# The second mixer's block inverse on packed 32x32 diagonal blocks, four products side by side in the array

## Chip, core and metric

One Trainium2 chip, one of its cores, one launch. The engines are PE (TensorE, matrix products into PSUM), DVE (VectorE), ACT (ScalarE), POOL (GpSimd) and SP (which issues most DMAs). Each runs its own instruction list in order and they meet only at semaphores. The metric is the device time of one launch in microseconds; lower is better.

## What is computed

Two transformer blocks on 256 tokens of width 1024, in float32. The change touches one part of the second block, the RWKV-7 mixer, whose core is a recurrence for each of 8 heads of width 64:

```
def step(state, inp):
    r_t, w_t, k_t, v_t, a_t, b_t = inp
    sa = jnp.einsum('bhvk,bhk->bhv', state, a_t)
    state = (state * w_t[:, :, None, :]
             + sa[..., :, None] * b_t[:, :, None, :]
             + v_t[..., :, None] * k_t[:, :, None, :])
    y_t = jnp.einsum('bhvk,bhk->bhv', state, r_t)
    return state, y_t
```

The kernel works in chunks of 64 tokens. Within a chunk the rows `sa` depend on each other through a strictly triangular 64x64 matrix M (one for each head and chunk), and are had at once by the inverse of I - M, a unit triangular matrix.

## The kernel before, in words

There are 4 chunks and 8 heads, so 32 matrices of 64x64. Two heads share the 128 partitions (head h on partitions 64h to 64h+63), so they lie as 16 units side by side: `m_b` holds M, `x_inv` and `xt_inv` hold the growing inverse and its transpose, both 128 x 16 x 64.

The inverse is grown by levels. At level 0 DVE sets `xt_inv` to the 2x2 blocks of M on the diagonal plus the identity (two operations, L1074 and L1077), PE turns it into `x_inv` (L578) and ACT copies that out of PSUM. At level n (1 to `LEVELS` = 5) blocks of size 2^n are joined in pairs: with N the part of M between the two (M times a mask in `levels`, by POOL, L1433, into `half_n`), P = N X (`first_product`), then X += X P and Xᵀ += Pᵀ Xᵀ (`second_product`). Level 5 needs only the transposed one. Every product is done for two halves f of 8 units, through `product` (L588): 8 units times 2 heads, so 16 matmuls of 64x64 with 64 columns into one PSUM bank. A head's matmul uses the 64 rows and the 64 columns of the array that its partitions stand for. In float32 a matmul shows as two records in the trace.

Round it goes PE -> ACT (P out of bank 4 into `half_1`, L861) -> PE -> DVE (`grow`: adds to `x_inv`, L1088, and `xt_inv`, L1091) -> PE. So that PE has something to do meanwhile, the level loop weaves in pieces of wide projections (`columns(...)`, L2196 to L2198, 3 matmuls of 128x128 by 256 columns for each step): after `first_product(n, 0)` stands `second_product(n - 1, 1)`, then `second_product(n, 0)`, `first_product(n, 1)`, and a piece of `columns`. These wide matmuls need each chunk of weights in two parts, which ACT (`split`, L1464, `w_hi`) and DVE (`split`, L1766, `w_lo`) make, in their own order between the level's operations. After the inverse comes the recurrence over chunks (L657), which uses `xt_inv`.

The masks are made once by POOL in `second_constants`, in the first block.

Of the kernel before, what the change touches and what calls it, by code (L numbers as in the profile page):

```python
# [10 lines left out]
ALU = mybir.AluOpType  # L11
ACT = mybir.ActivationFunctionType
# [26 lines left out]
NCH = T // CHUNK  # L39
LORA = 160  # L40
# [48 lines left out]
def block_pair(nc, inp, out, scratch, shifted):  # L89

    ctx = ExitStack()
    with ctx:
# [249 lines left out]
        x_inv, xt_inv = region(4096, NCH * HT, CHUNK), region(5120, NCH * HT, CHUNK)  # L342
        m_b, m_k = region(6144, NCH * HT, 2 * CHUNK), region(9216, NCH * HT, 2 * CHUNK)
        b_tok, k_tok, v_tok = (region(11264 + 1024 * j, NCH * HT, CHUNK) for j in range(3))
        half_1, half_n = region(14336, 2, 8 * CHUNK), region(15360, 2, 8 * CHUNK)
# [9 lines left out]
        levels = sb("levels", [P, 6, CHUNK])  # L355
        eye = sb("eye", [P, CHUNK])
# [37 lines left out]
        LEVELS = 5  # L394
        FUNITS = HT * TT
# [7 lines left out]
        def second_constants(told, pool, g):  # L403
# [20 lines left out]
            for h in range(2):  # L424
                a, b = HD * h, HD * (h + 1)
                g.tensor_copy(eye[a:b, :], ident[a:b, a:b]).then_inc(S["pool_step"], told.one("pool_step"))
                pool.wait_ge(S["pool_step"], told.value("pool_step"))
# [6 lines left out]
            for n in range(LEVELS + 1):  # L434
                w = 2 ** n
                both = levels[:, n, :].rearrange("p (b t) -> p b t", t=2 * w)
                g.memset(both[:, :, w:2 * w], 1.0).then_inc(S["pool_step"], told.one("pool_step"))
                pool.wait_ge(S["pool_step"], told.value("pool_step"))
                for h in range(2):
                    v = both[HD * h:HD * (h + 1)]  # L440
                    blocks = CHUNK // (2 * w)
# [4 lines left out]
                    done = "masks_ready" if n == LEVELS and h else "pool_step"  # L446
# [13 lines left out]
        def head(v, h, *rest):  # L460
            return v[(slice(HD * h, HD * (h + 1)), *rest)]


        def pe_mixer(told, pe, state, by_columns, by_tokens, by_rows, rows_to_tokens, turn_late_half, spread):
# [111 lines left out]
            for u in range(NCH * HT):  # L576
                for h in range(2):
# [7 lines left out]
            def product(b, left, right, f):  # L585
                for i in range(8):
                    for h in range(2):
# [4 lines left out]
            def x_of(f, i, h):  # L592
                return head(x_inv, h, 8 * f + i)

            def xt_of(f, i, h):
                return head(xt_inv, h, 8 * f + i)

            def n_of(f, i, h):
                return head(half_n, h, f, slice(i * CHUNK, (i + 1) * CHUNK))

            def p_of(f, i, h):
                return head(half_1, h, f, slice(i * CHUNK, (i + 1) * CHUNK))

            def first_product(n, f):

                done = 2 * (n - 1) + f
                pe.wait_ge(S["off_ready"], done + 1)
# [4 lines left out]
                product(4, n_of, x_of, f).then_inc(S["p1"], told.one("p1"))  # L612

            def second_product(n, f):

                done = 2 * (n - 1) + f
                pe.wait_ge(S["p1_copied"], done + 1)
                if n > 1:
                    pe.wait_ge(S["xt_added"], done - 1)
                if n < LEVELS:  # L620
                    product((6, 5)[f], xt_of, p_of, f)
                product((7, 3)[f], p_of, xt_of, f).then_inc(S["p2"], told.one("p2"))

            pe.wait_ge(S["turned_copied"], 8)
            pe.wait_ge(S["turned_copied"], 6)
# [20 lines left out]
            for c in range(NCH):  # L646
# [140 lines left out]
        def act_mixer(told, act, a, split, spread, state):  # L787
# [59 lines left out]
            copies("units_turned", 4, x_inv, 6, "turned_copied")  # L847
# [86 lines left out]
        def dve_mixer(told, dve, v, split, diagonals, out_bank, state):  # L934
# [139 lines left out]
            v.tensor_tensor(xt_inv, m_b[:, :, 0:CHUNK], over(levels[:, 0, :], NCH * HT), ALU.mult).then_inc(  # L1074
                S["dve_step"], told.one("dve_step"))
            dve.wait_ge(S["dve_step"], told.value("dve_step"))
            v.tensor_tensor(xt_inv, xt_inv, over(eye[:], NCH * HT), ALU.add).then_inc(  # L1077
# [5 lines left out]
            def grow(n, f):  # L1083

                dve.wait_ge(S["p2"], 2 * (n - 1) + f + 1)
                if n < LEVELS:
                    o = flat(x_inv[:, 8 * f:8 * f + 8, :])
                    v.tensor_tensor(o, o, bank[(6, 5)[f]][:, :], ALU.add).then_inc(  # L1088
                        S["x_added"], told.one("x_added"))
                o = flat(xt_inv[:, 8 * f:8 * f + 8, :])  # L1090
                v.tensor_tensor(o, o, bank[(7, 3)[f]][:, :], ALU.add).then_inc(  # L1091
                    S["xt_added"], told.one("xt_added"))

            dve.wait_ge(S["turned_copied"], 8)
# [235 lines left out]
        def _(pool):  # L1330
# [97 lines left out]
            pool.wait_ge(S["xt_first"], 1)  # L1428
            for n in range(1, LEVELS + 1):
                for f in range(2):  # L1430
                    if n > 1:
                        pool.wait_ge(S["p1"], 2 * (n - 2) + f + 1)
                    g.tensor_tensor(half_n[:, f, :].rearrange("p (u s) -> p u s", u=8),  # L1433
                                    m_b[:, 8 * f:8 * f + 8, 0:CHUNK], over(levels[:, n, :], 8), ALU.mult).then_inc(
                        S["off_ready"], told.one("off_ready"))

# [1121 lines left out]
```

## Time and profile before

| | us |
|---|---|
| median of 3 runs | 1129.97 (1129.5 to 1130.15) |
| the profiled execution's own time | 1129.57 |
| its span in the trace | 1127.7 |
| PE busy | 1116.1 (99%) |
| DVE busy | 768.8 (68%) |
| ACT busy | 559.5 (50%) |
| POOL busy | 183.4 (16%) |
| mean granted TensorE clock (share of 2.4 GHz) | 0.998 |

Times in the trace are microseconds from the span's start. A busy PE is a PE with a matmul in its pipeline; neighbouring matmuls overlap, so the time that one takes from the stream is the distance between starts, not its duration. The inverse lies between 752 and 803 us.

### The profile page before, as it was taken

How to read it: one execution, taken by the hardware profiler on the slowest of the kernel's cores; microseconds unless marked ns; L12 is line 12 of the kernel's file. 1: busy time of each engine (PE TensorE's matmuls, PEld its weight loads, DVE VectorE, ACT ScalarE, POOL GpSimd, SP SyncE). 2: the span in 40 equal slices, each digit the busy share in tenths (PEclk: the TensorE clock that was granted, in tenths of full speed). 3: DMA queues.
4: the chain of work that ended last, by engine and by line, in shares of the span. 5: the costliest groups of instructions: out<-in, count | busy, mean ns of one | idle time of the engine just before them, and what ended most of it. 6: DMA issues, size and time to landing. Idle time of an engine off the chain costs nothing.

```text
span 1127.7 us, 22169 instructions
## 1 busy us (share of the span) xinstructions
PE 1116.1 (99%) x9610; PEld 1058.4 (94%) x9610; DVE 768.8 (68%) x1033; ACT 559.5 (50%) x671; POOL 183.4 (16%) x127
## 2 busy tenths in 40 slices
PE   9999999999999999999999999999999999999997
PEld 9999999998999999899999999999998989999996
DVE  4988978757786776775555567974278675554554
ACT  6433344494754554674444448622245656343343
POOL 3888783000000000000000010113030010000000
PEclk9999999999999999999999999999999999999999
DMA  8586553355456555546456565433144354655551
GB/s 271 188 289 201 184 187 112 117 211 174 138 197 203 201 170 186 178 147 215 156 186 210 161 202 157 129 92 99 41 142 136 136 182 155 205 185 187 187 185 39
DMA packets 147150, 190.01 MB, mean 168 GB/s; under 512 B 7659, under 2 KB 132139, under 8 KB 146943
## 3 DMA queue, kind: packets, MB, share of 16 engines
q1 hardware_dynamic: 145743, 184.32, 50.2%
q0 software_dynamic: 1264, 4.55, 1.2%
q8 instruction: 59, 0.97, 0.4%
q14 instruction: 20, 0.16, 0.0%
q10 hardware_dynamic: 64, 0.02, 0.0%
HBM read 187.79 MB, written 2.65 MB: 169 GB/s over the span
## 4 chain that ended last, share of the span: by engine, by line
PE 94%; DVE 3%; ACT 2%; issue 1%; ACTq 0%; DVEq 0%
PE bank L2196 22%; PE bank L2197 21%; PE bank L2198 21%; PE bank L2348 6%; PE bank L2349 6%; PE bank L2350 6%; PE bank L588 2%; PE bank L657 1%; DVE w_lo L1766 1%; PE bank L2280 1%; PE bank L2276 1%; PE bank L2436 1%; PE bank L562 1%; PE bank L2450 1%; PE bank L475 0%
## 5 line engine op out<-in xcount | busy, mean ns | idle before, releaser
L2196 PE MATMUL bank<-X_hi,w_hi 128*128 128x256 f32 x1760 | 502.5, 286 | 0.6 <-DVE w_lo L1766 0.5
L2197 PE MATMUL bank<-X_lo,w_hi 128*128 128x256 f32 x1760 | 497.9, 283 | 0.0
L2198 PE MATMUL bank<-X_hi,w_lo 128*128 128x256 f32 x1760 | 497.9, 283 | 0.0
L1464 ACT ACTIVATE w_hi<-w_raw 128x2048 fp32r<-128x2048 f32 x170 | 324.0, 1909 | 149.6 <-PE bank L2198 112.4
L1766 DVE TENSOR_TENSOR w_lo<-w_raw,w_hi 128x2048 fp32r<-128x2048 f32 x144 | 332.4, 2311 | 42.4 <-ACT w_hi L1464 42.0
L2196 PEld LDWEIGHTS bank<-X_hi,w_hi 128*128 128x128 f32 x1760 | 337.3, 192 | 6.3 <-issue 2.6
L2197 PEld LDWEIGHTS bank<-X_lo,w_hi 128*128 128x128 f32 x1760 | 337.4, 192 | 1.2
L2198 PEld LDWEIGHTS bank<-X_hi,w_lo 128*128 128x128 f32 x1760 | 337.3, 192 | 0.0
L1893 DVE TENSOR_TENSOR arena<-bank,rstd 128x512 f32<-128x512 f32 x66 | 45.6, 691 | 184.3 <-PE bank L2198 179.5
L1373 POOL TENSOR_TENSOR w_lo<-w_raw,w_hi 128x2048 fp32r<-128x2048 f32 x23 | 106.8, 4650 | 33.0 <-ACT w_hi L1464 32.9
L2348 PE MATMUL bank<-w_hi,Y_hi 128*128 128x512 f32 x264 | 103.3, 391 | 1.2 <-DVE Y_lo L1921 1.2
L2349 PE MATMUL bank<-w_hi,Y_lo 128*128 128x512 f32 x264 | 103.1, 390 | 0.0
L2350 PE MATMUL bank<-w_lo,Y_hi 128*128 128x512 f32 x264 | 102.7, 389 | 0.0
L1415 POOL TENSOR_TENSOR w_lo<-w_raw,w_hi 128x2048 fp32r<-128x2048 f32 x2 | 9.2, 4596 | 537.4 <-ACT w_hi L1464 537.4
L1998 DVE SCALAR_TENSOR_TENSOR bank<-arena,par,bank 128x256 f32<-128x256 f32 x232 | 93.2, 482 | 0.6
L2348 PEld LDWEIGHTS bank<-w_hi,Y_hi 128*128 128x128 f32 x264 | 49.7, 188 | 11.1 <-DVE Y_lo L1921 1.6
L2350 PEld LDWEIGHTS bank<-w_lo,Y_hi 128*128 128x128 f32 x264 | 49.6, 188 | 10.6
L1574 ACT ACTIVATE arena<-arena,par 128x256 f32<-128x256 f32 x44 | 24.1, 595 | 69.4 <-DVE arena L1893 69.4
L2349 PEld LDWEIGHTS bank<-w_hi,Y_lo 128*128 128x128 f32 x264 | 49.7, 188 | 9.1
L1583 ACT ACTIVATE arena<-arena 128x512 f32<-128x512 f32 x22 | 13.9, 633 | 84.4 <-DVE arena L1893 84.4
L1597 ACT ACTIVATE Y_hi<-arena 128x512 fp32r<-128x512 f32 x33 | 20.9, 632 | 44.0 <-DVE arena L1914 44.0
L1803 DVE TENSOR_TENSOR arena<-bank,rstd 128x512 f32<-128x512 f32 x43 | 29.5, 687 | 13.7 <-PE bank L2198 9.9
(302 smaller groups left out, 1404.5 us busy)
## 6 DMA issues: line engine op xcount, KB each, us to landing
w_raw<-in_ffn_w_dram SPq DMA_DIRECT2D x66, 1024.0 KB, 5.4
w_raw<-in_w_in_dram SPq DMA_DIRECT2D x52, 1024.0 KB, 5.2
w_raw<-in_w_up_dram SPq DMA_DIRECT2D x22, 1024.0 KB, 5.1
w_raw<-in_w_down_dram SPq DMA_DIRECT2D x11, 1024.0 KB, 4.9
w_raw<-in_w_out_dram SPq DMA_DIRECT2D x8, 1024.0 KB, 5.1
w_raw<-in_conv_pw_w_dram SPq DMA_DIRECT2D x4, 1024.0 KB, 5.1
w_raw<-in_w_attn_out_dram SPq DMA_DIRECT2D x2, 1024.0 KB, 4.9
w_raw<-in_rwkv_proj_dram SPq DMA_DIRECT2D x2, 1024.0 KB, 4.9
```

Of the source, the lines that this page charges most:

```text
L1373: g.tensor_tensor(w_lo[n % RING][:, :], raw[n % RING][:, :], w_hi[n % RING][:, :].bitcast(F32), ALU.subtract).then_inc(S["w_lo_pool"], tol ...
L1464: a.activation(w_hi[slot][:, :], raw[slot][:, :], ACT.Copy).then_inc(S["w_hi"], told.one("w_hi"))
L1766: v.tensor_tensor(w_lo[slot][:, :], raw[slot][:, :], w_hi[slot][:, :].bitcast(F32), ALU.subtract).then_inc(S["w_lo"], told.one("w_lo"))
L1803: v.tensor_tensor(dst, pairs(b), over(rstd[:], 2), ALU.mult).then_inc(S[f"bank{b}_read"], 1)
L1893: v.tensor_tensor(u_t[:, side].rearrange("p (m t) -> p m t", m=2), pairs(2 * (i % 2) + side), over(rstd[:], 2), ALU.mult).then_inc(S[name] ...
L1998: v.scalar_tensor_tensor(out=conv[:, t, :] if k == CONV_W - 1 else part, in0=src, scalar=w, in1=part, op0=ALU.mult, op1=ALU.add).then_inc( ...
L2196: pe.matmul(o, wh, xh, start=start, stop=False, skip_group_check=True)
L2197: pe.matmul(o, wh, xl, start=False, stop=False, skip_group_check=True)
L2198: return pe.matmul(o, wl, xh, start=False, stop=stop, skip_group_check=True)
L2348: pe.matmul(o, yh, wh, start=first and k == 0, stop=False, skip_group_check=True)
L2349: pe.matmul(o, yl, wh, start=False, stop=False, skip_group_check=True)
L2350: mm = pe.matmul(o, yh, wl, start=False, stop=last, skip_group_check=True)
```

## The change

The inverse is grown to 32x32 only, on packed diagonal blocks, and the last level is done apart.

- Each 64x64 matrix has two 32x32 blocks on the diagonal. They lie on partitions 32q to 32q+31 (q = 0 to 3; two heads, two blocks each). POOL copies them out of `m_b` into a new `m_blocks` (128 x 16 x 32), 8 copies of 32 partitions by 256 elements. `x_blocks` and `xt_blocks` (128 x 16 x 32) replace `x_inv` and, up to level 4, `xt_inv`.
- Levels 1 to 4 run on these. `product` now makes, for each unit, 4 matmuls of 32x32 with 32 columns, each on its own 32 rows and its own 32 columns of the array, instead of 2 of 64x64 with 64 columns. The copies, adds and masks around them have half as many elements for each partition.
- Level 5 is `corner_product`: the 32x32 corner between the two blocks, 2 matmuls of 32x32 for each unit and product, no mask. DVE copies the corner into `xt_inv` (2 copies of 32 partitions for each half f in place of one add); POOL clears the opposite corner and copies the diagonal blocks into `xt_inv` (2 memsets, 8 copies). The recurrence waits for these at chunks 0 and 2.
- The turn before level 1 becomes 64 matmuls of 32x32 in place of 32 of 64x64, into one bank, and ACT copies one bank in place of two.
- The masks are 32 wide: 5 levels by 4 quarters in place of 6 levels by 2 halves.

```diff
-            for u in range(NCH * HT):
-                for h in range(2):
-                    mm = pe.matmul(head(bank[6 + u // 8], h, slice(u % 8 * CHUNK, u % 8 * CHUNK + CHUNK)),
-                                   head(xt_inv, h, u), head(ident, h, slice(HD * h, HD * (h + 1))),
-                                   start=True, stop=True)
+                for q in range(QUADRANTS):
+                    mm = pe.matmul(quadrant(bank[6], q, slice(u * BLOCK, (u + 1) * BLOCK)), quadrant(xt_blocks, q, u),
+                                   quadrant(ident, q, slice(q * BLOCK, (q + 1) * BLOCK)), start=True, stop=True)
...
             def product(b, left, right, f):
                 for i in range(8):
+                    for q in range(QUADRANTS):
+                        mm = pe.matmul(quadrant(bank[b], q, slice(i * BLOCK, (i + 1) * BLOCK)), left(f, i, q),
+                                       right(f, i, q), start=True, stop=True)
+                return mm
...
+            def corner_product(b, left, right, below, f):
+                for i in range(8):
                     for h in range(2):
-                        mm = pe.matmul(head(bank[b], h, slice(i * CHUNK, (i + 1) * CHUNK)), left(f, i, h),
-                                       right(f, i, h), start=True, stop=True)
+                        mm = pe.matmul(quadrant(bank[b], 2 * h + below, slice(i * BLOCK, (i + 1) * BLOCK)),
+                                       left(f, i, h), right(f, i, 2 * h + 1 - below), start=True, stop=True)
                 return mm
...
+                if c % 2 == 0:
+                    pe.wait_ge(S["off_ready"], 2 * QUADRANTS + 2 * (LEVELS - 1) + QUADRANTS * (c // 2 + 1))
...
-                    a.activation(half_1[:, f, :], bank[4][:, :], ACT.Copy).then_inc(
+                    a.activation(half_1[:, f, :], bank[4][:, 0:T], ACT.Copy).then_inc(
...
+            dve.wait_ge(S["off_ready"], 2 * QUADRANTS)
+            v.tensor_tensor(xt_blocks, m_blocks, over(levels[:, 0, :], NCH * HT), ALU.mult).then_inc(
...
+                    for h in range(2):
+                        done = "xt_added" if h else "dve_step"
+                        v.tensor_copy(quadrant(xt_inv, 2 * h, slice(8 * f, 8 * f + 8), slice(BLOCK, CHUNK)),
...
+            for f in range(2):
+                pool.wait_ge(S["masked"], 4 * f + 3)
+                for q in range(QUADRANTS):
+                    g.tensor_copy(quadrant(m_blocks, q, units(f)), quadrant(m_b, q, units(f), diagonal_block(q))).then_inc(
+                        S["off_ready"], told.one("off_ready"))
...
+            for f in range(2):
+                pool.wait_ge(S["xt_added"], 2 * (LEVELS - 2) + f + 1)
+                for q in range(QUADRANTS):
+                    g.tensor_copy(quadrant(xt_inv, q, units(f), diagonal_block(q)),
+                                  quadrant(xt_blocks, q, units(f))).then_inc(S["off_ready"], told.one("off_ready"))
```

What this makes of the instruction lists, at two places. First PE in level 2, before: the four lines are `first_product(2, 0)`, `second_product(1, 1)`, `second_product(2, 0)` and `first_product(2, 1)`, each with its first matmul apart.

```order
3916 L588 MATMUL bank<-arena 64x64 [waits x_added,p1_copied,off_ready]
3917 L588 MATMUL bank<-arena 64x64 x15
3918 L588 MATMUL bank<-arena 64x64 [waits p1_copied]
3919 L588 MATMUL bank<-arena 64x64 x31
3920 L588 MATMUL bank<-arena 64x64 [waits xt_added,p1_copied]
3921 L588 MATMUL bank<-arena 64x64 x31
3922 L588 MATMUL bank<-arena 64x64 [waits x_added,p1_copied,off_ready]
3923 L588 MATMUL bank<-arena 64x64 x15
```

And the same place of the changed kernel:

```order
3916 L597 MATMUL bank<-arena 32x32 [waits x_added,p1_copied,off_ready]
3917 L597 MATMUL bank<-arena 32x32 x31
3918 L597 MATMUL bank<-arena 32x32 [waits p1_copied]
3919 L597 MATMUL bank<-arena 32x32 x63
3920 L597 MATMUL bank<-arena 32x32 [waits xt_added,p1_copied]
3921 L597 MATMUL bank<-arena 32x32 x63
3922 L597 MATMUL bank<-arena 32x32 [waits x_added,p1_copied,off_ready]
3923 L597 MATMUL bank<-arena 32x32 x31
```

Order and waits stay; there are twice as many matmuls, each a quarter of the size. The second place is POOL round the inverse. Before (L1415 is a weight split in the first block's feed-forward part, L1433 the masks times M, L1439 the forgetting rows of the attention):

```order
94 L1426 DMA bias_by_distance<-arena 8x256 [waits forget]
95 L1433 TENSOR_TENSOR arena<-arena,levels 128x512 [waits xt_first]
96 L1433 TENSOR_TENSOR arena<-arena,levels 128x512
97 L1433 TENSOR_TENSOR arena<-arena,levels 128x512 [waits p1] x8
98 L1439 DMA arena<-bias_by_distance 128x2048 [waits y_summed,forget_stored]
```

After:

```order
108 L1466 DMA bias_by_distance<-arena 8x256 [waits forget]
109 L1479 COPY arena<-arena 32x256 [waits masked]
110 L1479 COPY arena<-arena 32x256 x3
111 L1479 COPY arena<-arena 32x256 [waits masked]
112 L1479 COPY arena<-arena 32x256 x3
113 L1486 TENSOR_TENSOR arena<-arena,levels 128x256 [waits off_ready]
114 L1486 TENSOR_TENSOR arena<-arena,levels 128x256
115 L1486 TENSOR_TENSOR arena<-arena,levels 128x256 [waits p1] x6
116 L1492 MEMSET arena 32x16x32 [waits off_ready,xt_first]
117 L1492 MEMSET arena 32x16x32
118 L1498 COPY arena<-arena 32x8x32 [waits xt_added,pool_step]
119 L1498 COPY arena<-arena 32x8x32 x3
```

Eight copies now stand ahead of the first mask, and DVE's first two operations of the inverse, which waited only for PE and ACT before, wait for them as well; eight more copies and two memsets stand behind the last mask.

## Rows read from the trace of the kernel before

**Rows 1.** The page: busy time of PE, and the chain that ended last.
```profile
PE 1116.1 (99%) x9610; PEld 1058.4 (94%) x9610; DVE 768.8 (68%) x1033; ACT 559.5 (50%) x671; POOL 183.4 (16%) x127
...
PE 94%; DVE 3%; ACT 2%; issue 1%; ACTq 0%; DVEq 0%
```

**Rows 2.** Timeline of PE: start us, us, engine, line, operation, shapes, records.
```profile
754.98 2.08 PE L578 MATMUL bank<-ident,arena 64*64 64x64 f32 x64
756.99 0.39 PE L2196 MATMUL bank<-X_hi,w_hi 128*128 128x256 f32 x1
...
759.34 1.15 PE L588 MATMUL bank<-arena 64*64 64x64 f32 x32
760.42 0.39 PE L2196 MATMUL bank<-X_hi,w_hi 128*128 128x256 f32 x1
...
766.62 5.82 PE L588 MATMUL bank<-arena 64*64 64x64 f32 x192
772.36 0.39 PE L2196 MATMUL bank<-w_hi,X_hi 128*128 128x256 f32 x1
...
803.26 14.41 PE L657 MATMUL bank<-arena 64*64 64x64 f32 x432
```

**Rows 3.** Timeline of PE elsewhere: other shapes and pairs of tiles (rows*columns of the array).
```profile
692.84 0.37 PE L515 MATMUL bank<-arena 32*128 32x256 f32 x1
692.84 0.37 PE L517 MATMUL bank<-arena 32*128 32x256 f32 x1
...
721.62 0.61 PE L540 MATMUL bank<-ident,arena 8*128 8x8 f32 x4
...
741.34 7.20 PE L562 MATMUL bank<-arena 64*64 64x128 f32 x128
...
819.94 1.89 PE L697 MATMUL bank<-arena,head_ones 128*128 128x256 f32 x8
```

**Rows 4.** Timeline of ACT, of the inverse and of the recurrence behind it.
```profile
764.39 0.60 ACT L861 ACTIVATE arena<-bank 128x512 f32<-128x512 f32 x1 [3.26 <-PE bank L588]
764.88 1.91 ACT L1464 ACTIVATE w_hi<-w_raw 128x2048 fp32r<-128x2048 f32 x1
...
803.99 0.38 ACT L868 ACTIVATE arena<-bank 128x256 f32<-128x256 f32 x1 [1.77 <-PE bank L657]
```

**Rows 5.** Timeline of DVE: the first steps of the inverse, level 2, a 128x256 add.
```profile
749.32 2.29 DVE L1766 TENSOR_TENSOR w_lo<-w_raw,w_hi 128x2048 fp32r<-128x2048 f32 x1
751.52 0.68 DVE L1803 TENSOR_TENSOR arena<-bank,rstd 128x512 f32<-128x512 f32 x1
...
753.65 1.23 DVE L1077 TENSOR_TENSOR arena<-arena,eye 128x1024 f32<-128x1024 f32 x1
...
766.82 2.29 DVE L1766 TENSOR_TENSOR w_lo<-w_raw,w_hi 128x2048 fp32r<-128x2048 f32 x1 [2.02 <-ACT w_hi L1464]
769.03 0.68 DVE L1803 TENSOR_TENSOR arena<-bank,rstd 128x512 f32<-128x512 f32 x1
769.75 0.69 DVE L1088 TENSOR_TENSOR arena<-arena,bank 128x512 f32<-128x512 f32 x1
...
810.35 0.42 DVE L1107 TENSOR_TENSOR arena<-arena,bank 128x256 f32<-128x256 f32 x1 [3.54 <-PE bank L657]
```

**Rows 6.** Timeline of POOL: the masks of the inverse, and two places in the first block.
```profile
156.62 0.74 POOL L1395 TENSOR_TENSOR sq<-sq 128x256 f32<-128x256 f32 x1
...
183.14 4.14 POOL L1403 TENSOR_TENSOR sq<-sq 128x512 f32<-128x512 f32 x3 [6.41 <-ACT sq L1470]
...
760.58 1.29 POOL L1433 TENSOR_TENSOR arena<-arena,levels 128x512 f32<-128x512 f32 x1 [1.05 <-PE bank L588]
...
767.86 2.38 POOL L1433 TENSOR_TENSOR arena<-arena,levels 128x512 f32<-128x512 f32 x1 [2.12 <-PE bank L588]
```

**Rows 7.** Stretch 735 to 805 us: busy us (records); its instruction queue: packets, MB.
```profile
735.00:805.00 70.00, 69.98 (x1533) 67.62 (x1533) 39.25 (x49) 18.75 (x27) 16.42 (x10) 1.00 0.29 91
...
q8 instruction: 12, 0.20, 1.2%
```

More of the change, by code:

```diff
@@ L39 @@
 NCH = T // CHUNK
+BLOCK = 32
 LORA = 160
@@ L433, in second_constants @@
                     pool.wait_ge(S["pool_step"], told.value("pool_step"))
-            for n in range(LEVELS + 1):
+            for q in range(QUADRANTS):
+                c = slice(BLOCK * q, BLOCK * (q + 1))
+                g.tensor_copy(eye[c, :], ident[c, c]).then_inc(S["pool_step"], told.one("pool_step"))
+            pool.wait_ge(S["pool_step"], told.value("pool_step"))
+            for n in range(LEVELS):
                 w = 2 ** n
@@ L438, in second_constants @@
                 pool.wait_ge(S["pool_step"], told.value("pool_step"))
[L439 to L441 removed]
+                for q in range(QUADRANTS):
+                    v = both[BLOCK * q:BLOCK * (q + 1)]
+                    blocks = BLOCK // (2 * w)
                     g.affine_select(out=v, in_=v, compare_op=ALU.is_ge, fill=0.0, base=0,
@@ L445, in second_constants @@
                     pool.wait_ge(S["pool_step"], told.value("pool_step"))
-                    done = "masks_ready" if n == LEVELS and h else "pool_step"
+                    done = "masks_ready" if n == LEVELS - 1 and q == QUADRANTS - 1 else "pool_step"
                     g.affine_select(out=v, in_=v, compare_op=ALU.is_ge, fill=0.0, base=w - 1,
@@ L611, in first_product @@
                     pe.wait_ge(S["x_added"], done - 1)
-                product(4, n_of, x_of, f).then_inc(S["p1"], told.one("p1"))
+                if n < LEVELS:
+                    mm = product(4, n_of, x_of, f)
+                else:
+                    mm = corner_product(4, corner_of, x_of, 1, f)
+                mm.then_inc(S["p1"], told.one("p1"))
             def second_product(n, f):
@@ L621, in second_product @@
                     product((6, 5)[f], xt_of, p_of, f)
-                product((7, 3)[f], p_of, xt_of, f).then_inc(S["p2"], told.one("p2"))
-            pe.wait_ge(S["turned_copied"], 8)
-            pe.wait_ge(S["turned_copied"], 6)
+                    mm = product((7, 3)[f], p_of, xt_of, f)
+                else:
+                    mm = corner_product((7, 3)[f], p_below, xt_of, 0, f)
+                mm.then_inc(S["p2"], told.one("p2"))
+            pe.wait_ge(S["turned_copied"], 7)
             pe.wait_ge(S["forget_read"], 1)
@@ L846, in act_mixer @@
             copies("units_turned", 3, v_tok, 4, "turned_copied")
-            copies("units_turned", 4, x_inv, 6, "turned_copied")
+            act.wait_ge(S["units_turned"], 4)
+            a.activation(flat(x_blocks), bank[6][:, :], ACT.Copy).then_inc(
+                S["turned_copied"], told.one("turned_copied"))
             def v_tokens(j):
@@ L1073, in dve_mixer @@
             dve.wait_ge(S["units_turned"], 2)
-            v.tensor_tensor(xt_inv, m_b[:, :, 0:CHUNK], over(levels[:, 0, :], NCH * HT), ALU.mult).then_inc(
+            dve.wait_ge(S["off_ready"], 2 * QUADRANTS)
+            v.tensor_tensor(xt_blocks, m_blocks, over(levels[:, 0, :], NCH * HT), ALU.mult).then_inc(
                 S["dve_step"], told.one("dve_step"))
             dve.wait_ge(S["dve_step"], told.value("dve_step"))
-            v.tensor_tensor(xt_inv, xt_inv, over(eye[:], NCH * HT), ALU.add).then_inc(
+            v.tensor_tensor(xt_blocks, xt_blocks, over(eye[:], NCH * HT), ALU.add).then_inc(
                 S["xt_first"], told.one("xt_first"))
@@ L1432, in _ @@
                         pool.wait_ge(S["p1"], 2 * (n - 2) + f + 1)
-                    g.tensor_tensor(half_n[:, f, :].rearrange("p (u s) -> p u s", u=8),
-                                    m_b[:, 8 * f:8 * f + 8, 0:CHUNK], over(levels[:, n, :], 8), ALU.mult).then_inc(
+                    g.tensor_tensor(half_n[:, f, :].rearrange("p (u s) -> p u s", u=8), m_blocks[:, units(f), :],
+                                    over(levels[:, n, :], 8), ALU.mult).then_inc(
                         S["off_ready"], told.one("off_ready"))
+            pool.wait_ge(S["xt_first"], 1)
+            pool.wait_ge(S["off_ready"], told.value("off_ready"))
+            for h in range(2):
+                g.memset(quadrant(xt_inv, 2 * h + 1, slice(0, NCH * HT), slice(0, BLOCK)), 0.0).then_inc(
+                    S["pool_step"], told.one("pool_step"))
+            pool.wait_ge(S["pool_step"], told.value("pool_step"))
+            for f in range(2):
+                pool.wait_ge(S["xt_added"], 2 * (LEVELS - 2) + f + 1)
+                for q in range(QUADRANTS):
+                    g.tensor_copy(quadrant(xt_inv, q, units(f), diagonal_block(q)),
+                                  quadrant(xt_blocks, q, units(f))).then_inc(S["off_ready"], told.one("off_ready"))
             pool.wait_ge(S["forget_stored"], 16)
```

63 lines of the change are left out of this document (39 added, 24 removed).

## The prediction

> **What bounds the kernel now.** I read the page's busy times and the chain that ended last first [rows 1]: PE is busy for 99% of the span and holds 94% of the chain, so what leaves PE's stream shortens the launch, and what happens on DVE, ACT and POOL counts only where PE comes to wait for it. Then PE's timeline through the inverse [rows 2]. The blocks of small matmuls and the wide ones follow each other without a hole: the block of level 2 (192 records) starts at 766.62, and the next wide matmul at 772.36, 5.74 us later; a block of 32 records takes 760.42 - 759.34 = 1.08 us. So a record costs (5.74 - 1.08) / 160 = 29.1 ns and a block 1.08 - 32 x 0.0291 = 0.15 us for going in and out. Each record has a partner, the other head's, so I count in steps: one pass of all tiles of a unit. A step is 58.3 ns. The records of L588 are 896, so 448 steps; the turn (L578) has 64 records, 32 steps. In all 480 steps and 28.0 us of step time, everything else being wide matmuls that stay.
>
> **What a step costs after.** The number of steps does not change. In levels 1 to 4 (384 steps) and in the turn (32) a step now has four tiles in place of two, and the corner level (64 steps) has two tiles, all 32x32 with 32 columns. So the change is worth 480 times the difference between 58.3 ns and the new step P, and P is the number to find. No row has a 32x32 tile with 32 columns. Three shapes bound it [rows 2, 3]:
> - 64 weight columns, 64 moving columns: 58 ns (L588).
> - 64 weight columns, 128 moving columns: (7.20 - 0.15) / 64 = 110 ns for a pair (L562).
> - 128 weight columns, 8 moving columns: (0.61 - 0.25) / 3 = 120 ns, where 0.25 is my estimate for the last one's pipeline time (L540).
>
> So the larger of the two counts sets the time, by 0.052 us for each 64 columns above 58 ns. Halving both should take off half of that, 26 ns: P = 32 ns. That is so if four tiles overlap as two do. For the two: L515 and L517 stand on different rows of the array and start at the same 692.84 [rows 3], and a pair of L562 with 128 columns each takes 110 ns, where one matmul of the full array needs (1.89 - 0.38) / 7 = 216 ns for 256 columns, 108 for 128 (L697) [rows 3]. Two tiles thus cost what one costs. Four are not in the trace. The lower bound is P = 27, half of the bare 53 ns by which the other shapes differ; the upper is that records come no denser than the densest stream of this trace, one in 29.1 ns, 116 ns for four and 58 for two. I take 32, as the stagger in a pair is too small to be seen in rows of a hundredth of a microsecond, so four fit in.
>
> A rule that speaks against this: the Trainium skill, in "TensorEngine Tiling (Array Packing)", under "Restrictions and Gotchas", says that different row tiles cannot access the same PSUM bank at the same time, and all four quarters write one bank here. By it four would be done one after another, and the step would be 4 x 32 = 128 ns. But L562's and L588's two heads are different row tiles and share a bank, and the 110 ns for two speaks against it, as long as they write different partitions.
>
> **The sum on PE.** 480 x (58.3 - 32) = -12.6 us: the turn -0.8, levels 1 to 4 -10.1, the corner -1.7. The 9 blocks keep their 0.15 us each.
>
> **What may now wait.** The cover is shorter, so I put the loop on a clock again.
> - ACT's copy of P has half the elements: 0.38 us in place of 0.60 [rows 4]. It begins some 0.2 us after the last matmul of `first_product(n, 0)`, and is covered by `second_product(n - 1, 1)`, 32 steps or 1.0 us: 0.6 needed, no wait. At level 1 the cover is 0.9 us of wide matmuls, enough.
> - DVE's adds take 0.42 us each in place of 0.69 [rows 5]. `first_product(n, 1)` needs `x_added` of (n - 1, 1), with `second_product(n, 0)` between, 1.0 us: 0.2 + 0.42 needed, no wait by themselves.
> - But between the adds DVE has `split`, and at level 1 also L1803. From ACT's split at 764.88 to DVE's split (766.82), L1803 (769.03) and the add at 769.75 with its end at about 770.4 [rows 4, 5], it is one chain of 5.5 us, and only 0.25 us of it shrinks. It starts when ACT has copied P of (1, 1). New clock: the turn starts at 754.98 as before and ends 0.8 earlier, so level 1's first block starts at 758.5 and lasts 16 x 0.032 + 0.15 = 0.66 us (before 1.08). With the same 0.9 us of wide matmuls the second block (48 steps) starts at 760.1 and ends at 761.8. ACT's copy follows at 761.9, its split at 762.2, and the chain's add is done at 762.2 + 5.25 = 767.5. PE: 2.35 us of wide matmuls, level 2's block from 764.1, and the 80 steps ahead of `first_product(2, 1)` end at 764.1 + 0.1 + 2.6 = 766.8. PE waits **0.8 us** there. Before, this add was done at 770.4 and PE came to it at 766.62 + 0.1 + 80 x 0.058 = 771.4. Levels 3 and 5 have no L1803 in the chain, and their chain starts 3 us of wide matmuls ahead; it ends with the last product of the level's first half or before it: no wait. This is what is late next; if P is lower, it grows by a step's difference times 80.
> - POOL, now ahead of DVE's first two steps. The copies for the first half of the units run before 748, the second four start at about 748.5 (when the last `m_b` is masked). A 128x256 operation on POOL takes 0.74 us with two inputs; I estimate 0.5 for a copy. POOL does not get on while DVE makes a `w_lo`: L1433 took 2.38 us at 767.86, when DVE's split ran to 769.1, and 1.29 at 760.58, when none did [rows 5, 6]. DVE's split from 749.32 to 751.6 [rows 5] thus pushes two or three of the four copies behind it: done at 752.6 to 753.2, against 752.4, when DVE was ready before. The masks of level 1 now follow at once on POOL, 0.74 us each, and can hold DVE up in turn. Against this DVE's two operations take half of 1.23 us each [rows 5]. They ended at 754.88 and would now end between 754.0 and 755.6; PE wants them at 754.98. I take **0.3 us** (0 to 1).
> - At the end PE went from the last block over 0.9 us of wide matmuls into the recurrence at 803.26 [rows 2]. The last block is short now, and DVE has two copies of about 0.4 us in place of one add of 0.69: **0.1 us**.
> - The copies into `xt_inv` on POOL: the first four can start in level 4, the second in level 5, some 5 us ahead of the recurrence for 2 us of work (4 x 0.5). Hidden by that; uncovered it would be up to 2 us.
> - Masks on POOL in the first block: 50 operations where there were 36, smaller ones. The 6.41 us for which POOL waited at 183.14 [rows 6] cover them.
> - Behind the inverse PE and the splits keep their distances, so what is won stays won.
>
> Sum: -12.6 + 0.8 + 0.3 + 0.1 = -11.4 us, from 1129.57 for the profiled execution 1118.2; the median of the runs lies 0.4 higher, so **1118.6 us**. Own range of this case: 1115 (P = 27 and a longer wait at level 2) to 1121.
>
> **Rivals.**
> 1. *Four tiles do not come as densely as two.* For each step of four PE needs four weight loads and four matmuls in 32 ns, twice as many instructions for each step as now and near four times the present rate. Nothing in the trace shows PE fed at that rate. The instruction queue moved 12 packets of 0.20 MB in these 70 us for 1533 matmul records, 128 each, in 1.2% of 16 engines' time, so 1.1 us each [rows 7]; a level's block of 384 records would now want 3 of them in 3.1 us, just what one queue gives. Halfway, P = 45 for the 416 steps of four: 416 x 13 = 5.4 us less gain, but the wait at level 2 goes too: 1123.5. Chance 0.17, range 1121 to 1128.
> 2. *PE takes a record at a time at a fixed pace* (the other side). That the present 29.1 ns for a record were a pace, not 64 columns, is against L562's 55 ns and the shared starts of L515 and L517, yet no row has a denser stream. Then four tiles cost 116 ns and two stay at 58: 416 x 58.3 = +24.3, no gain at the corner, no waits: 1154. It turns from gain to loss at P = 62 for four (with the corner's 1.7 us kept). Chance 0.12, range 1132 to 1154. The Trainium skill has a floor of that kind, in "TensorE: Matmul & The Clock Gate", section "Wait — 56ns, not 53.3ns?": starts never closer than about 25 ns, however few the columns. By it a step of four would be 100 ns, and the time 416 x 42 = 17 us above 1130, about 1147. L515 and L517, with one start on different rows of the array, speak against it between tiles.
> 3. *Only two tiles overlap.* Four make 2 x 32 = 64 ns: 416 x 5.7 = +2.4, the corner -1.7: 1130.7, no change. The present pairs are all that the trace shows. Chance 0.07.
> 4. *Waits eat more*: DVE and POOL take turns at more places than I counted, and each level's adds come late by a microsecond: 1123. It falls in the range of rival 1; chance 0.06.
>
> **How the numbers follow.** The likeliest case has 0.58 and gives 1118.6. The range leaves out rival 2 and half of the third: 1114.5 to 1130.5. A change under 0.2% (2.3 us) is about what a measurement of this kernel can't tell from none. Faster: the first case, 1 and 4, 0.81, less 0.03 for the tail of 1: 0.78. Same: 0.03 and most of rival 3: 0.09. Slower: 0.13.
>
> **What would show it.** In the trace of the changed kernel the block of level 2 to 4 should take 96 x 0.032 + 0.15 = 3.2 us where it took 5.74 (level 2 with a hole of 0.8 us before its last quarter, levels 3 and 4 without). L588's successor has 1664 records, in blocks of 0.66 us (64 records) and 1.0 us in the corner level. DVE's second step of the inverse ends by 755.6. ACT's copies take 0.38 us. If the block takes over 5.7 us, rival 2 or 3 holds; if it is between 3.5 and 5 without a wait named, rival 1; if waits of PE for DVE stand at every level, rival 4. I am wrong, too, if the wide matmuls take longer than before, or if the gain is there at 803 us and gone at the end.

## The result and the profile after

| | before | after |
|---|---|---|
| median, us | 1130.06 (6 runs) | 1150.19 (6 runs, 1147.27 to 1152.62) |
| profiled execution, us | 1129.57 | 1149.05 |
| its span, us | 1127.7 | 1147.0 |
| mean granted TensorE clock | 0.998 | 0.987 |

The changed kernel is slower: the ratio of the times is 1.018, 95% interval 1.017 to 1.019. That is 20 us lost where 11 us of gain were forecast.

Nearly all of it lies in the inverse: 18.2 of the 19.3 us by which the two profiled spans differ. From the turn to the recurrence PE took 803.26 - 754.98 = 48.3 us before; after, it takes 822.15 - 755.65 = 66.5. The 0.67 us by which the later trace starts the inverse late are there at 742 us already, and behind the recurrence the two run alike to 0.4 us.

PE's timeline shows what no row of before has, a stream that breaks off. These are the small matmuls of levels 1 to 3 (L597 is `product`, L588's successor; the last bracket is the idle time ahead, "issue" meaning that PE waited for nothing that the profile shows). They answer to the L588 rows of [rows 2]:

```profile
765.29 1.32 PE L597 MATMUL bank<-arena 32*32 32x32 f32 x128 [0.43 <-issue]
768.59 0.63 PE L597 MATMUL bank<-arena 32*32 32x32 f32 x40 [1.98 <-issue]
...
772.86 1.95 PE L597 MATMUL bank<-arena 32*32 32x32 f32 x197
777.15 1.35 PE L597 MATMUL bank<-arena 32*32 32x32 f32 x127 [2.33 <-issue]
780.72 1.06 PE L597 MATMUL bank<-arena 32*32 32x32 f32 x60 [2.23 <-issue]
```

A full piece between two holes has 127 or 128 records, whatever product it belongs to. While a piece runs, it runs as forecast: 128 records, 32 steps of four tiles, in 1.32 us less about 0.19 for the last one's pipeline time, 35 ns a step. Then PE has nothing to do for some 2 us. PE's list of waits between 741 and 830 us (us in total, times, longest) says it in three lines; the kernel before has no line at all in this list between 741 and 811 us:

```profile
PE bank L597 <- issue: 15.7, 8, 3.6
PE bank L588 <- issue: 2.2, 1, 2.2
PE bank L2260 <- issue: 0.7, 1, 0.7
```

The wide matmuls behind a hole are slow too. Before, their starts are 0.12 us apart and each lasts 0.28; these are the first ones behind level 2's block:

```profile
781.72 0.58 PE L2260 MATMUL bank<-w_hi,X_hi 128*128 128x256 f32 x1
782.10 0.42 PE L2261 MATMUL bank<-w_lo,X_hi 128*128 128x256 f32 x1
782.31 0.41 PE L2262 MATMUL bank<-w_hi,X_lo 128*128 128x256 f32 x1
```

They start 0.21 us apart. The stretches of the two kernels from the turn to the recurrence (columns: stretch, then busy us and records of PE, PE's weight loads, DVE, ACT and POOL, granted clock, DMA share, GB/s) first after, then before:

```profile
754.98:822.15 67.17, 48.52 (x1943) 45.51 (x1942) 18.65 (x27) 12.35 (x20) 8.57 (x16) 0.80 0.24 76
```

```profile
754.98:803.26 48.28, 48.28 (x1106) 46.48 (x1105) 22.49 (x24) 14.46 (x20) 16.39 (x10) 1.00 0.32 98
```

PE is idle for 18.7 us of it, and the granted clock has a mean of 0.80: with levels 2.4 and 1.2 GHz that is 40% of the stretch at 1.2. Summing the distances between PE's starts by kind gives the whole account. A hole is counted here from the start of the last matmul ahead of it to the next start, so each is about 0.2 us longer than the idle time in brackets:

| us in this stretch | before | after | difference |
|---|---|---|---|
| small matmuls | 28.0 | 18.2 | -9.8 |
| holes | 0 | 20.6 | +20.6 |
| wide matmuls | 17.1 | 24.4 | +7.3 |
| going in and out of blocks | 3.2 | 3.3 | +0.1 |
| sum | 48.3 | 66.5 | +18.2 |

### The profile page after: what moved, and what is told of

Its sections match the earlier page's. It is cut to its first block, busy times and chain, and to the rows that moved or that the text cites. A ratio compares the mean times of both kernels' runs of the same rounds, so it can differ in the third digit from the quotient of the medians.

```text
span 1147.0 us, 23869 instructions
## 1 busy us (share of the span) xinstructions
PE 1116.3 (97%) x10442; PEld 1057.6 (92%) x10442; DVE 764.8 (67%) x1035; ACT 556.7 (49%) x670; POOL 187.1 (16%) x160
## 4 chain that ended last, share of the span: by engine, by line
PE 93%; DVE 3%; issue 2%; ACT 2%; ACTq 0%; DVEq 0%
PE bank L2260 21%; PE bank L2261 21%; PE bank L2262 21%; PE bank L2412 6%; PE bank L2413 6%; PE bank L2414 6%; PE bank L597 2%; PE bank L686 1%; DVE w_lo L1830 1%; PE bank L2344 1%; PE bank L2340 1%; PE bank L2500 1%; PE bank L572 1%; PE bank L2514 1%; PE bank L485 0%
## 5 line engine op out<-in xcount | busy, mean ns | idle before, releaser
L1957 DVE TENSOR_TENSOR arena<-bank,rstd 128x512 f32<-128x512 f32 x66 | 45.6, 691 | 184.2 <-PE bank L2262 179.4
L2414 PEld LDWEIGHTS bank<-w_lo,Y_hi 128*128 128x128 f32 x264 | 49.6, 188 | 10.5
L2260 PE MATMUL bank<-w_hi,X_hi 128*128 128x256 f32 x128 | 39.3, 307 | 0.7 <-issue 0.7
```

The lines of the kernel that those rows point to most:

```text
L1957: v.tensor_tensor(u_t[:, side].rearrange("p (m t) -> p m t", m=2), pairs(2 * (i % 2) + side), over(rstd[:], 2), ALU.mult).then_inc(S[name] ...
L2260: pe.matmul(o, wh, xh, start=start, stop=False, skip_group_check=True)
L2414: mm = pe.matmul(o, yh, wl, start=False, stop=last, skip_group_check=True)
```

## The experiments

Two theories of the holes. S: PE's instructions are supplied at a limited pace, 128 matmul records a packet, and four tiles use them up faster. T: the tiles; PE cannot keep four 32x32 tiles at work, or it stops after some number of them. A third question is the clock: do the holes lower it (C1), or the small tiles (C2)?

### Four tiles where nothing else is going on

```diff
             feed(2)
+            pe.wait_ge(S["tile_summed"], told.value("tile_summed"))
+            for i in range(160):
+                for q in range(4):
+                    pe.matmul(bank[1][32 * q:32 * (q + 1), i % 8 * 32:i % 8 * 32 + 32], ident[32 * q:32 * (q + 1), 32 * q:32 * (q + 1)],
+                              ones[32 * q:32 * (q + 1), 0:32], start=True, stop=True)
```

> The kernel before with 160 steps of four 32x32 tiles (1280 records) put on PE behind its last product, where nothing waits for it and the DMA queues move only the output. Theory S: the burst runs at about 9 ns a record for as long as instructions are at hand (one or two packets, 128 to 256 records), then stops every 128 records for about 2 us; 1280 records last about 10 x 3.6 = 36 us less the first, so the launch ends 25 to 30 us later, and the instruction packets come 3.5 us apart although no weights are moved. If the holes of the changed kernel came from DMA traffic or from its waits on other engines, the burst runs without holes, 12 us.

Measured: 1158.51 us, one run. PE's timeline (columns as above) has the same pieces and holes behind the kernel's last product, with no semaphore in between and no weights on the way (the output, 1.05 MB, is written in the first 9 us):

```profile
1120.68 2.12 PE L2538 MATMUL bank<-ones,ident 32*32 32x32 f32 x229
1125.45 1.27 PE L2538 MATMUL bank<-ones,ident 32*32 32x32 f32 x128 [2.65 <-issue]
1130.29 1.93 PE L2538 MATMUL bank<-ones,ident 32*32 32x32 f32 x128 [3.57 <-issue]
...
1145.06 1.93 PE L2538 MATMUL bank<-ones,ident 32*32 32x32 f32 x128 [1.55 <-issue]
1148.54 1.93 PE L2538 MATMUL bank<-ones,ident 32*32 32x32 f32 x128 [1.55 <-issue]
```

From 1145.06 to 1148.54 it is 3.48 us a piece. The granted clock is 1.00 up to 1125 us and 0.50 from 1130 us on, so a late piece runs for 1.93 us where the one at 1125.45 took 1.27. The DMA queues between 1120 and 1157 us (packets, MB, share of 16 engines' time):

```profile
GB/s 0 111 173 18 0 120 383 334 31 0 0 0 18 0 0 0 18 0 0 0 18 0 0 0 18 0 0 0 18 0 0 0 18 0 0 18 0 0 0 0
...
q8 instruction: 9, 0.15, 1.7%
```

In the line of 40 slices of 0.93 us, once the output is written (the peak at 383), one slice in four shows 18 GB/s: one packet of 16 KB for each piece of 128 records. Nine packets in 1.7% of 16 engines' 37 us are 1.1 us each. The trace has the times of single packets too, and with them the 3.48 us come apart. The piece at 1145.06 starts; 1.1 us later, at 1146.17, the next packet starts and is under way for 0.93 us; 1.4 us after its end, at 1148.54, the next piece starts. So a packet sets off only when PE has begun on the one before it. The changed kernel does the same in its stretch from 803 to 811 us, where no weights are on the way (40 slices of 0.2 us):

```profile
GB/s 0 0 0 0 0 0 0 0 82 0 0 0 0 0 0 0 0 0 0 0 0 0 0 0 0 82 0 0 0 0 0 0 0 0 0 0 0 0 0 0
...
q8 instruction: 2, 0.03, 1.5%
```

Its pieces start at 803.62 and 806.90, the two packets at 804.72 and 808.01, again 1.1 us behind. The first of these pieces runs at full clock, and it is 3.28 us to the next: the pace is 3.3 to 3.5 us a packet.

The same times settle what ends a hole. In the changed kernel all ten end 1.2 to 1.5 us after the end of an instruction packet. In this run and in the three further ones below that keep the small tiles of levels 1 to 4 it is 1.2 to 1.6 us for all 32 that the profile puts to "issue". Where PE waits for ACT instead (the run with ACT held, below), the last packet had ended 0.8, 4.4, 2.4, 1.5 and 7.5 us before. Nothing of the changed kernel's waits, of its transfers or of its other engines is needed for the holes.

### As many instructions in tiles of 64x64

```diff
+            for i in range(320):
+                for h in range(2):
+                    pe.matmul(bank[1][64 * h:64 * (h + 1), i % 8 * 64:i % 8 * 64 + 64], ident[64 * h:64 * (h + 1), 64 * h:64 * (h + 1)],
+                              ones[64 * h:64 * (h + 1), 0:64], start=True, stop=True)
```

> The kernel before with 320 steps of two 64x64 tiles (1280 records, as many instructions as in the burst of four tiles) put on PE behind its last product. Theory S: at 58.3 ns a step 128 records take 3.73 us, longer than the 3.5 us in which a packet comes, so there is no hole and the burst takes 320 x 0.058 = 18.7 us (the clock stays full), about 11 us past the end of before, near 1141. If any long run of small matmuls brings holes, the launch ends at 1158 as with four tiles.

Measured: 1159.79 us, one run. The burst has no hole, as S says, and its length was worked out wrongly in the expectation: 1280 records of two tiles are 640 steps, not 320, so 37.3 us. The time alone would have spoken for the other side (1158 us); it is the trace that decides.

```profile
1120.15 37.55 PE L2538 MATMUL bank<-ones,ident 64*64 64x64 f32 x1280
...
q8 instruction: 10, 0.16, 1.8%
```

(Timeline, and the instruction queue from 1120 to 1158 us.) 128 records of this kind take 37.55 / 10 = 3.75 us, just over the 3.3 to 3.5 in which a packet comes. So the kernel before ran its blocks some 10% below the pace at which instructions come. Its trace shows packets as close as 3.66 us and no hole, so it could not tell how much closer they can come.

### The changed kernel's matmuls, two tiles at a time

```diff
-                for i in range(8):
-                    for q in range(QUADRANTS):
+                for i, q in [(i, q) for pair in ((0, 2), (1, 3)) for i in range(8) for q in pair]:
```

> The changed kernel with the same matmuls in another order: in each product of levels 1 to 4 first the quarters 0 and 2 of all 8 units, then 1 and 3, so two tiles are at work at a time in place of four and a product has twice as many steps. Theory S: the instructions are as many, so the supply sets the time: 1148 to 1152, no change against the changed kernel, with holes that are shorter, since a block of 128 records runs for 2.1 us in place of 1.2. Theory T (PE cannot hold four tiles at a time): the holes go; with 32 ns for a step of two, 16 ns a record, levels 1 to 4 take 1536 x 16 = 25 us and the time is about 1133.

Measured: 1153.44 us, 1.0211 of before (1.0195 to 1.0226). Two tiles in place of four make 3 us of difference, not the gain of 17 us that T says (the time lies 1.4 us above the range that S gave): the holes are still there after 127 or 128 records, 15.4 us of waiting in place of 18.6, though not each of them is shorter (timeline of PE, level 2):

```profile
772.81 2.76 PE L596 MATMUL bank<-arena 32*32 32x32 f32 x197
777.14 1.96 PE L596 MATMUL bank<-arena 32*32 32x32 f32 x127 [1.57 <-issue]
782.14 1.63 PE L596 MATMUL bank<-arena 32*32 32x32 f32 x60 [3.04 <-issue]
```

From 772.81 to 777.14 it is 4.3 us, like the 4.3 from 772.86 to 777.15 in the changed kernel. The time follows how many instructions there are, and hardly how many tiles work at once. T falls.

### Half of the products left out

```diff
-                for i in range(8):
+                for i in range(4):
                     for q in range(QUADRANTS):
```

> The changed kernel with the products of levels 1 to 4 made for 4 of the 8 units of each half only, four 32x32 tiles a step: the other units' products are left out, so 768 records where the changed kernel has 1536, and as many as the kernel before. Theory S: 192 records for each level and 24 wide matmuls, 216 in some 5.5 us, a demand near the supply (128 in 3.6 us is 216 in 6.1 us): a level takes about 6 us in place of 12.5, holes under 1 us, and no half clock; time 1150 less 4 levels of 6 us and the half clock, 1116 to 1122. Theory T: holes of 2 us after each 128 records stay as they are, with half of them, and wide matmuls at half clock: 1130 to 1140.

Measured: 1127.01 us, 0.9976 of before (0.9966 to 0.9986). Half the small records take away 23 us, of which the work left out is about 7 (192 steps of 35 ns). That is 5 us above the range of S and below that of T. Holes are fewer (10.0 us in five, one of them not for instructions, where the changed kernel has 20.6 in ten), but they do not shrink to under 1 us, as S with my figures said: the turn alone still costs 2.7 us, and behind a hole the clock is at 1.2 GHz. With all the products of levels 1 to 4 in fast tiles and half of them left out, the kernel is only 2.9 us faster than the one before. One wait of another kind comes to light here, now that PE reaches it before it runs dry:

```profile
769.01 1.72 PE L597 MATMUL bank<-arena 32*32 32x32 f32 x160
772.52 0.65 PE L597 MATMUL bank<-arena 32*32 32x32 f32 x32 [1.79 <-DVE arena L1122]
```

That is `first_product(2, 1)` waiting for DVE's add behind `split` and the other operation of level 1, the chain that the prediction put at 0.8 us.

### The same instructions, spread out

```diff
                 first_product(n, 0)
+                if 1 < n < LEVELS:
+                    piece = (0, 0, 0, 4, 0)[n]
+                    columns(B_FOX + 4 + n // 4, tokens=True, steps=(piece, piece + 1))
...
                     second_product(n - 1, 1)
+                if 1 < n < LEVELS:
+                    columns(B_FOX + 4 + n // 4, tokens=True, steps=(piece + 1, piece + 2))
...
                 second_product(n, 0)
+                if 1 < n < LEVELS:
+                    columns(B_FOX + 4 + n // 4, tokens=True, steps=(piece + 2, piece + 3))
```

> The changed kernel with the same instructions in another order: in levels 2 to 4 the wide matmuls of the level stand in four pieces behind each product, in place of in one piece behind the last. Theory S (supply of 128 records in 3.5 to 3.6 us, with one or two packets ahead): a level's 384 small and 24 wide records need 3.2 packets, 11.3 us at the least, and now come near that, where the changed kernel took 13.8, 14.7 and some 12.5 us: 4 to 6 us less, 1144 to 1146, still far above the kernel before. If the holes hung on the length of a dense block alone (96 to 128 records in a piece now), they would go, and the time would be 1120 to 1125.

Measured: 1149.37 us, 1.0164 of before (1.0146 to 1.0183). The holes do not hang on the length of a block. But the 4 to 6 us that better use of the supply should have given are not there either: level 2 takes 784.33 - 773.01 = 11.3 us, as worked out, level 3 takes 14.5. PE's waits for "issue" add up to more than in the changed kernel:

```profile
PE bank L597 <- issue: 18.1, 10, 3.8
PE bank L588 <- issue: 2.5, 1, 2.5
```

So spreading does not help, and the length of a single hole (up to 3.8 us here, 3.6 in the changed kernel, 1.6 in the quiet burst) isn't explained by the pace alone. The packet times point at the other transfers. In the burst a packet starts 1.1 to 1.2 us behind the start of the piece before it, seven times out of eight; the eighth stands 2.4 us behind, while the output is written, and the hole is 3.57 us. The changed kernel's longest hole, 3.65 us up to 791.98, is alike: PE had begun on the last block at 787.0, the packet started at 789.64, 2.6 us later, and from 787.4 on 1 MB of weights was on the way (786 to 792 us, slices of 0.15 us):

```profile
GB/s 0 0 0 0 0 0 0 0 0 89 143 123 123 177 307 362 335 403 375 396 369 403 362 403 485 355 369 348 382 328 225 75 14 7 7 14 20 20 27 20
```

That a packet comes late because of these transfers is read from their coincidence; no run moves the weights to test it.

### Holes without small tiles

The kernel before, with ACT held ahead of its copy of P for the first half of each level:

```diff
                     act.wait_ge(S["p1"], 2 * (n - 1) + f + 1)
+                    if f == 0:
+                        for _ in range(10):
+                            a.activation(spare[:], ident[:, :], ACT.Copy).then_inc(S["act_step"], told.one("act_step"))
+                            act.wait_ge(S["act_step"], told.value("act_step"))
```

> The kernel before, its 64x64 products and all its matmuls as they were, with ACT held for 10 small copies (some 2.5 to 3 us) ahead of its copy of P in the first half of each of the 5 levels, so that PE has 5 holes of about 1.5 to 2.5 us. Theory C1 (the half clock of the changed kernel came from the holes in PE's work): the granted clock falls to 1.2 GHz after such holes here too, and wide matmuls take 0.21 us a start in place of 0.12. Theory C2 (it came from the 32x32 tiles, which keep little of the array at work): the clock stays at 2.4 GHz; the time is then that of before plus 5 holes, 1138 to 1142, and with C1 a few us above that.

Measured: 1145.88 us, one run. Every matmul is of the shapes of before, and the clock falls behind the holes all the same. Timeline of PE in level 2, then the stretch from 778 to 780 us (granted clock third from the end):

```profile
776.86 4.19 PE L590 MATMUL bank<-arena 64*64 64x64 f32 x96 [2.24 <-ACT arena L867]
780.98 0.58 PE L2202 MATMUL bank<-w_hi,X_hi 128*128 128x256 f32 x1
781.36 0.41 PE L2203 MATMUL bank<-w_lo,X_hi 128*128 128x256 f32 x1
781.57 0.36 PE L2204 MATMUL bank<-w_hi,X_lo 128*128 128x256 f32 x1
781.77 0.28 PE L2202 MATMUL bank<-w_hi,X_hi 128*128 128x256 f32 x1
```

```profile
778.00:780.00 2.00, 2.00 (x52) 2.00 (x48) 0.62 (x2) 0.00 (x0) 0.00 (x0) 0.58 0.33 104
```

Ninety-six records that take 3.02 us at full clock take 4.19 here. Not every hole does it (behind the one of level 3, of the same 2.24 us, they took 3.02 again). So holes are enough to lower the clock, as C1 says. Whether long runs of small tiles lower it too, as C2 says, is not shown: in every run the clock first falls in a hole or behind one, and the kernels without holes have few small tiles (mean clock 0.998 to 1.000). The five holes are 11.8 us together, counted from start to start; the other 4 of the 16 us by which this kernel is longer go to matmuls at 1.2 GHz.

### The part of the change that adds no instructions

The kernel before with the corner alone: levels 1 to 4 on 64x64, level 5 in two tiles of 32x32 a step.

```diff
+            def corner_first(f):
+                for i in range(8):
+                    for h in range(2):
+                        mm = pe.matmul(quadrant(bank[4], 2 * h + 1, slice(i * BLOCK, (i + 1) * BLOCK)),
+                                       quadrant(m_b, 2 * h, 8 * f + i, slice(BLOCK, CHUNK)),
+                                       quadrant(x_inv, 2 * h, 8 * f + i, slice(0, BLOCK)), start=True, stop=True)
+                return mm
...
-                product(4, n_of, x_of, f).then_inc(S["p1"], told.one("p1"))
+                (product(4, n_of, x_of, f) if n < LEVELS else corner_first(f)).then_inc(S["p1"], told.one("p1"))
...
-                product((7, 3)[f], p_of, xt_of, f).then_inc(S["p2"], told.one("p2"))
+                (product((7, 3)[f], p_of, xt_of, f) if n < LEVELS else corner_second(f)).then_inc(
+                    S["p2"], told.one("p2"))
```

> The kernel before with one part of the change alone: levels 1 to 4 stay on 64x64, level 5 is done as the 32x32 corner (two tiles a step, the same number of records as before, no mask, two 32-partition copies by DVE). Theory S (PE's instructions are delivered no faster than 128 matmul records in about 3.6 us, a page at a time, and a block runs short when it needs them faster): no more instructions than before, the dense stretches have 32 or 64 records, so no hole; the corner's 64 steps cost 32 to 35 ns in place of 58, 1.5 us less, 1128.3 to 1128.9. Theory T (32x32 tiles themselves make PE stop or its clock fall): holes or a half clock in level 5, 1130 or more.

Measured: 1128.39 us, 0.9986 of before (0.9977 to 0.9995). As S says: faster by 1.5 us, no hole. Timeline of PE, the last block of the corner and the wide matmul behind it; from start to start that block takes 0.63 us, before it took 1.08:

```profile
800.62 0.69 PE L619 MATMUL bank<-arena 32*32 32x32 f32 x32
801.25 0.38 PE L2225 MATMUL bank<-X_hi,w_hi 128*128 128x256 f32 x1
```

From this grew a version that is faster still: at level 4 X is updated for the upper diagonal block only, which is all that the corner reads of it.

```diff
-                    product((6, 5)[f], xt_of, p_of, f)
+                if n < LEVELS - 1:
+                    product((6, 5)[f], xt_of, p_of, f)
+                elif n < LEVELS:
+                    top_product(f)
```

(`top_product`: 16 matmuls of 32x32, on quarters 0 and 2, in place of 16 of 64x64; DVE adds 32x32 blocks accordingly.)

> e1 (64x64 products, the corner alone as 32x32) and one more place with two 32x32 tiles and no more instructions: at level 4 the update of X is made for the upper diagonal block alone, since the corner needs no more of it. 32 steps at about 28 ns in place of 58: 1.0 us less than e1's 1128.4, so 1127.4. Theory S: these 64 records in two short runs are carried by the packets at hand, no hole, clock full. If DVE's three small adds in place of two hold up the next product, the gain shrinks to nothing: 1128.4.

Measured: 1127.18 us, 0.9978 of before (0.9969 to 0.9987), 2.5 us faster than before and 23 faster than the changed kernel.

## Why the prediction was wrong, step by step

- **The step of four tiles** was right in kind and nearly in size. Forecast 32 ns, between bounds of 27 and 116; in the changed kernel 32 steps take 1.13 us, 35 ns. Four tiles overlap, in one PSUM bank. The page's rule against that ("TensorEngine Tiling (Array Packing)" of the Trainium skill, "Restrictions and Gotchas"), under which a step would have cost 128 ns, is not what the trace shows, for matmuls that write different partitions.
- **The step that failed is the sum's silence on instruction supply**, and in it one number. The prediction saw the demand (3 packets in 3.1 us for a level's block) and priced the supply by the time that a packet is under way, 1.1 us [rows 7], "just what one queue gives". The runs show 3.3 to 3.5 us between packets when PE is waiting for them: 1.1 us until the packet sets off, 0.9 to 1.4 under way, 1.2 to 1.5 until PE runs on. The prediction's price was the middle part alone. A level's 408 records need 3.2 packets, 10.5 to 11 us, where 8.8 us were spent before and 6.3 were forecast; levels 2 to 4 took 13.8, 14.7 and 12.4. In the holes this made +20.6 us. The row could have warned of it: with 1533 records in 70 us a packet came once in 5.8 us on average and nowhere closer than 3.66, so it could not tell how fast they can come.
- **Rival 1** had the mechanism and gave it 5 us. **Rival 2** had the size: records no denser than one in 29.1 ns, "at a fixed pace", 1154; the pace is 3.3 to 3.5 us / 128 = 26 to 27 ns. That its time came out within 4 us is partly luck, as 7.3 us of the loss are the clock on wide matmuls, which it did not have. The pace holds on average over more than one or two packets and not from start to start, as within a piece records come 9 ns apart. The Trainium skill's floor of 25 ns ("TensorE: Matmul & The Clock Gate", "Wait — 56ns, not 53.3ns?") came out near that average and, by the same luck, near the time (1147 us), and does not describe what happens: a step of four takes 35 ns, not 100.
- **The clock** was not in the sum: +7.3 us on wide matmuls that the change does not touch, and the small ones were at 1.2 GHz for a part as well. They gained 9.8 us in place of 12.6; of the 2.8 us missing, 1.2 are the step's 35 ns in place of 32 (416 steps), the rest the clock. The wide matmuls behind a hole were named as what would make the prediction wrong.
- **The waits.** DVE's chain at level 2 (0.8 us forecast) was hidden in the changed kernel by the holes, and is there in the run with half of the products, with 1.79 us. POOL ahead of DVE's first two steps cost nothing: PE reached the turn 0.91 us after the start of the wide piece before it, in both kernels. POOL was held up, though. These are POOL's and DVE's rows, which answer to [rows 5, 6]:

```profile
749.14 3.85 POOL L1479 COPY arena<-arena 32x256 f32<-32x256 f32 x4 [1.75 <-DVE arena L1099]
753.07 1.86 POOL L1486 TENSOR_TENSOR arena<-arena,levels 128x256 f32<-128x256 f32 x2
```

```profile
753.12 1.22 DVE L1108 TENSOR_TENSOR arena<-arena,levels 128x512 f32<-128x512 f32 x1 [0.24 <-POOL arena L1479]
754.38 1.10 DVE L1111 TENSOR_TENSOR arena<-arena,eye 128x512 f32<-128x512 f32 x1
```

  Four copies take 3.85 us beside DVE's split where the first four took 1.75, and DVE's operations on half of the elements last about as long as before, 1.22 and 1.10; POOL's masks run at the same time, which is the likely reason, and no run takes them away. ACT's copies take 0.38 us, DVE's adds 0.42, as forecast.
- **The masks in the first block** stayed covered, narrowly: POOL waited 6.41 us behind them before [rows 6], and 0.82 now:

```profile
183.74 4.14 POOL L1443 TENSOR_TENSOR sq<-sq 128x512 f32<-128x512 f32 x3 [0.82 <-ACT sq L1534]
```

- **The corner**, -1.7 us with 0.1 for the last wait, measured alone as -1.5.

## To carry to other kernels

Count instructions before making matmuls smaller. Here a packet of 128 matmul records comes every 3.3 to 3.5 us at best, so once a run is longer than one or two packets a record costs 26 to 27 ns on average, however little it computes. Smaller tiles paid here only where the number of records stayed the same. A hole in PE's stream costs more than its length, since the clock may be at half behind it. And a row tells of a supply only what was asked of it: the duration of a transfer is no rate. To find what ended a hole marked "issue", look for the instruction packet that ended just before it.

## What the runs showed of the hardware that I had not expected

- PE's instruction queue had one packet of 16 KB, worth 128 matmul records, every 3.3 us (changed kernel, full clock) to 3.5 us (quiet burst, half clock) when PE was waiting for it and nothing else was on the way, though the packet itself is under way for about 1 us. It starts 1.1 us after PE has begun on the packet before it. The Trainium skill, "Runtime: NRT & Kernel Launch", section "Instruction fetch mechanics", has the blocks of 16 KiB and says that crossing into the next costs a step that is mostly hidden. The block size agrees (0.15 MB in 9 packets); that it is hidden does not hold here, with 1.6 us of each 3.5 idle in the quiet burst and 20.6 us of holes in the changed kernel.
- The burst had 229 records before its first hole, the rest of one packet and the whole of the next, so one packet is held ahead.
- Four tiles of 32x32 at 2.4 GHz take 35 ns a step, two of them 28 (64 records of the corner: 799.01 - 797.97 = 1.04 us, less 0.15), two of 64x64 58.
- PE's holes of 2.2 us were enough for the granted clock to fall to 1.2 GHz in some cases and not in others, in a kernel with no small tiles.
